# Two blocks on one core: merged activations turned by VectorE, low splits on GpSimd, memory rows scaled later

## The reference, cut to what matters

```python
merged = sigmoid(g_ret) * (o_ret @ w_ret_up) + sigmoid(g_moba) * (o_moba @ w_moba_up)
x = x + merged @ w_out
...
mkv = rms_norm(mem, mem_norm_g) @ w_mem_kv
...
merged = jnp.einsum('bsnd,bsnd->bsd', g, y_br)
x = x + merged @ w_out_2
```

## Time and profile before

| | |
|---|---|
| median of 3 runs | 2433.71 us (2433.43 to 2434.93) |
| the profiled execution, whole | 2433.67 us |
| its span, first to last instruction | 2431.8 us |
| PE busy | 2423.5 us, 100% of the span |
| PEld busy | 2000.7 us, 82% |
| DVE busy | 1682.1 us, 69% |
| ACT busy | 1241.7 us, 51% |
| POOL busy | 239.3 us, 10% |
| DMA | 464.20 MB, mean 191 GB/s |

### The profile page before, as it was taken

How to read it: one execution, slowest core, us unless ns; L and a number is a source line. 1 busy time by engine, 2 the same in 40 slices (tenths; PEclk the granted TensorE clock), 3 DMA queues, 4 the chain that set the end, 5 groups by cost and what they waited for, 6 DMA issues and landing times.

```text
span 2431.8 us, 34053 instructions
## 1 busy us (share of the span) xinstructions
PE 2423.5 (100%) x11017; PEld 2000.7 (82%) x11017; DVE 1682.1 (69%) x2171; ACT 1241.7 (51%) x1620; POOL 239.3 (10%) x250
## 2 busy tenths in 40 slices
PE   9999999999999999999999999999999999999999
PEld 7888888878888888888888878888887888888887
DVE  5467655587877988988888887454456645587564
ACT  5445454555455444444444445454556555655443
POOL 0022233231000000000000000010101100521000
PEclk9999999999999999999999999999999999999999
DMA  7655555576655655555555656855554545555655
GB/s 269 192 189 173 183 175 179 190 223 227 208 191 173 205 192 193 193 192 192 188 192 196 198 183 210 252 185 169 173 184 158 181 164 174 180 167 171 226 182 164
DMA packets 134822, 464.20 MB, mean 191 GB/s; under 512 B 14544, under 2 KB 21328, under 8 KB 134112
## 3 DMA queue, kind: packets, MB, share of 16 engines
q1 hardware_dynamic: 122464, 443.08, 55.6%
q10 hardware_dynamic: 12256, 20.15, 2.5%
q0 software_dynamic: 32, 0.03, 0.0%
HBM read 455.87 MB, written 7.34 MB: 190 GB/s over the span
## 4 chain that ended last, share of the span: by engine, by line
PE 98%; DVE 1%; issue 1%; ACT 0%; ACTq 0%; DVEq 0%
PE PS L646 21%; PE PS L648 21%; PE PS L647 21%; PE PS L893 7%; PE PS L894 7%; PE PS L895 7%; PE PS L913 3%; PE PS L915 3%; PE PS L914 3%; PE PS L758 1%; PE PS L728 1%; PE PS L687 1%; PE PS L708 0%; PE PS L736 0%; DVE WL L1640 0%
## 5 line engine op out<-in xcount | busy, mean ns | idle before, releaser
L1640 DVE TENSOR_TENSOR WL<-RAW,WH 128x1024 fp32r<-128x1024 f32 x842 | 1058.4, 1261 | 702.3 <-ACT WH L1118 693.8
L1118 ACT ACTIVATE WH<-RAW 128x1024 fp32r<-128x1024 f32 x841 | 889.1, 1059 | 1098.9 <-PE PS L648 721.9
L646 PE MATMUL PS<-WH,HT 128*128 128x512 f32 (+1 forms) x1816 | 718.5, 396 | 0.2 <-DVE WL L1640 0.2
L648 PE MATMUL PS<-WH,HT 128*128 128x512 f32 (+1 forms) x1816 | 706.5, 389 | 0.0
L647 PE MATMUL PS<-WL,HT 128*128 128x512 f32 (+1 forms) x1816 | 705.5, 388 | 0.0
L646 PEld LDWEIGHTS PS<-WH,HT 128*128 128x128 f32 x1816 | 341.1, 188 | 72.6 <-issue 5.4
L648 PEld LDWEIGHTS PS<-WH,HT 128*128 128x128 f32 x1816 | 340.8, 188 | 70.9
L647 PEld LDWEIGHTS PS<-WL,HT 128*128 128x128 f32 x1816 | 341.3, 188 | 67.3
L893 PE MATMUL PS<-WH,HT 128*128 128x512 f32 x704 | 274.3, 390 | 0.0
L895 PE MATMUL PS<-WH,HT 128*128 128x512 f32 x704 | 273.9, 389 | 0.0
L894 PE MATMUL PS<-WL,HT 128*128 128x512 f32 x704 | 273.9, 389 | 0.0
(11 more groups left out here) (306 smaller groups left out, 2114.7 us busy)
## 6 DMA issues: line engine op xcount, KB each, us to landing
RAW<-w_stream SPq DMA_DIRECT2D x841, 512.0 KB, 3.3
bias_scratch<-BE ACTq DMA_DIRECT2D x12, 256.0 KB, 4.0
MEMR<-mem_in ACTq DMA_DIRECT2D x1, 2048.0 KB, 10.5
X<-x_in ACTq DMA_DIRECT2D x4, 512.0 KB, 4.4
x_scratch<-X ACTq DMA_DIRECT2D x4, 512.0 KB, 4.5
X<-x_scratch ACTq DMA_DIRECT2D x1, 2048.0 KB, 11.3
out<-X ACTq DMA_DIRECT2D x8, 256.0 KB, 3.0
X<-x_in SPq DMA_DIRECT2D x3, 512.0 KB, 9.6
```

The costliest lines, as they stand in the source:

```text
L646: pe.matmul(o, hi, WH[:, slot, kk, 0:cols], start=k == 0, stop=False)
L648: ins = pe.matmul(o, lo, WH[:, slot, kk, 0:cols], start=False, stop=k == nq * GK - 1)
L1118: act.activation(WH[:, g.slot(j)], RAW[:, g.slot(j)], ACT.Copy).then_inc(hi_split, 1)
L1640: dve.tensor_tensor(WL[:, s], RAW[:, s], WH[:, s].bitcast(F32), ALU.subtract).then_inc(lo_split, 1)
```

## The change

**Turning.** The 64 identity products on `MERGED1` and `MERGED2`, and the steps that made them, are gone from TensorE's program. VectorE turns each chunk of 4 tiles after its `up_chunk`, with 16 transposes of 32x256 from `MERGED` into a new SBUF tensor `MT` (`merged_turn`, semaphore `merged_turned`). ScalarE copies the high parts from `MT` (`merged_hi`: at steps 7, 11 and 15 of the up stage for chunks 0 to 2, at step 4 of the out stage for chunk 3, each behind that step's split), and VectorE subtracts the low parts from `MT` (`merged_lo`: those of chunk c-1 between `up_chunk(c)` and `merged_turn(c)`, those of chunk 3 at the end). TensorE waits before each of the first 8 groups of the out stage for the low parts of the two tiles that the group needs.

**Low splits.** In each of the two up stages VectorE makes the low parts of the groups 4 to 7 first and then none until its chunks are done. GpSimd makes those of the next 17 groups (8 to 24, counted from the stage's first group; 16 to 24 are the first nine of the out stage). VectorE waits for them and goes on with group 25.

**Memory rows.** They are turned unscaled. The inverse roots go to `XR[:, 2:4]` and are applied by ScalarE when it copies the products of `mem0`, `mem1` and `mem2` out of PSUM: two instructions of 128x512 in place of one of 128x1024. The squares move from step 3 to step 4 and write their unused output to PSUM. Turning and splitting move 2 steps later (6 to 21, and 22 to 29). `mem0` waits tile by tile.

The core of the diff:

```diff
+        MT = sb("MT", [P, KT, S], F32, at_u1)
+        POOL_SPLITS = NCH * GW + 5
...
-            rstd(2, norm_ms, norm_rstd, 2)
+            def low_splits(name, first, end):
+                g = At(GROUP0[name])
+                for j in range(first + RING, end + RING):
+                    hold(hi_split, g.count(j + 1))
+                    hold(lo_split, g.count(j))
+                    s = g.slot(j)
+                    pool.tensor_tensor(WL[:, s], RAW[:, s], WH[:, s].bitcast(F32), ALU.subtract).then_inc(lo_split, 1)
+
+            low_splits("up_ret", GW, POOL_SPLITS)
+            rstd(2, norm_ms, norm_rstd, 2, XR[:, 2:4])
...
+            low_splits("up_b", GW, POOL_SPLITS)
...
+            def turned(name):
 
                 def before(p):
-                    if p in (0, 6):
-                        pe.wait_ge(tr_lo, TR[name] + (12 if p == 0 else KT))
-                return steps, before
-            straight("up_ret", NCH, GW, U[0], up_steps("merged1", 0))
-            steps, before = out_steps("merged1", 0)
+                    if p < GD:
+                        pe.wait_ge(tr_lo, TR[name] + 2 * p + 2)
+                return before
+            straight("up_ret", NCH, GW, U[0])
+            pe.sem_inc(tr_done, KT)
...
-            straight("out1", NCH, GD, HT, steps, before)
-            pe.wait_ge(mem_lo, KT)
-            straight("mem0", 1, GD, MEMT, mem0_steps)
+            straight("out1", NCH, GD, HT, None, turned("merged1"))
+            straight("mem0", 1, GD, MEMT, mem0_steps, lambda p: pe.wait_ge(mem_lo, 2 * p + 2))
...
+            def merged_hi(name, chunks, c):
+                act.wait_ge(merged_turned, chunks + c + 1)
+                for k in range(FT * c, FT * c + FT):
+                    act.activation(HT[:, k, 0, :], MT[:, k], ACT.Copy).then_inc(tr_hi, 1)
+
             for p in range(NCH * GW):
                 split(At(GROUP0["up_ret"]), p + RING)
...
-                transposed("merged1", HT, merged_tiles(p), None)
-                if p == 3:
+                if p % GW == GW - 1 and p > GW:
+                    merged_hi("merged1", 0, p // GW - 1)
+                if p == 4:
                     act.wait_ge(mem_loaded, 16)
-                    for t in range(T):
-                        ins = act.activation(JUNK[:, t, :], MEMR[:, t, :], ACT.Square, scale=D ** -0.5, accum_out=MS[:, t:t + 1])
-                    ins.then_inc(norm_ms, 1)
+                    mean_squares([(MEMR[:, t, :], XR[:, 2 + t:3 + t]) for t in range(T)], D ** -0.5, norm_ms)
...
             for p in range(NCH * GD):
                 split(At(GROUP0["out1"]), p + RING)
-                if p in (1, 2):
-                    transposed("merged1", HT, merged_tiles(NCH * GW + p), None)
+                if p == 4:
+                    merged_hi("merged1", 0, NCH - 1)
...
+            def merged_turn(merged, chunks, c):
+
+                dve.wait_ge(merged_ready, chunks + c + 1)
+                for a in range(4):
+                    for b in range(4):
+                        src = merged[32 * a:32 * a + 32].rearrange("p t (k d) -> p t k d", k=KT)[:, :, FT * c:FT * c + FT, 32 * b:32 * b + 32]
+                        dst = MT[32 * b:32 * b + 32].rearrange("p k (t s) -> p t k s", t=T)[:, :, FT * c:FT * c + FT, 32 * a:32 * a + 32]
+                        ins = dve.transpose(dst, src)
+                ins.then_inc(merged_turned, 1)
+
+            def merged_lo(name, c):
+
+                for k in range(FT * c, FT * c + FT):
+                    dve.wait_ge(tr_hi, TR[name] + k + 1)
+                    dve.tensor_tensor(HT[:, k, 1, :], MT[:, k], HT[:, k, 0, :].bitcast(F32), ALU.subtract).then_inc(tr_lo, 1)
+
+            def merged_chunks(stage, name, chunks):
+
+                for p in range(GW):
+                    split(At(GROUP0[stage]), p + RING)
+                for c in range(NCH):
+                    up_chunk(stage, MERGED[name], c)
+                    if c:
+                        merged_lo(name, c - 1)
+                    merged_turn(MERGED[name], chunks, c)
+                merged_lo(name, NCH - 1)
+
             dve.wait_ge(prod_free, 2 + PROD0["up_ret"])
...
+            merged_chunks("up_ret", "merged1", 0)
+            dve.wait_ge(lo_split, GROUP0["up_ret"] + POOL_SPLITS + RING)
...
-            for p in range(NCH * GD):
+            dve.wait_ge(mem_loaded, 16)
+            for p in range(POOL_SPLITS - NCH * GW, NCH * GD):
                 split(At(GROUP0["out1"]), p + RING)
...
-                if 4 <= p < 20:
-                    dve.wait_ge(norm_rows, 1)
-                    turn_memory((p - 4) // 4, (p - 4) % 4)
+                if 6 <= p < 22:
+                    turn_memory((p - 6) // 4, (p - 6) % 4)
```

More of the change, by code:

```diff
@@ L321, in build @@
         mem_turned = sem("mem_turned")
+        merged_turned = sem("merged_turned")
         mem_hi = sem("mem_hi")
@@ L1085, in _ @@
             pe.wait_ge(head_out, HEADS + 1)
[L1086 to L1088 removed]
+            straight("up_b", NCH, GW, U[2])
+            straight("out2", NCH - 1, GD, HT, None, turned("merged2"))
             g, n = At(GROUP0["out2"]), At(PROD0["out2"] + NCH - 1)
@@ L1150, in project @@
                         split(g, p + RING)
-                        evacuations(name, g, i, p, 2, dst, func, name in ("moba_proj", "ret_proj", "gates_ret"))
+                        evacuations(name, g, i, p, 2, dst, func, XR[:, 0:T] if name in ("moba_proj", "ret_proj", "gates_ret") else None)
                         if steps:
@@ L1372, in _ @@
                 g = At(GROUP0["mem0"])
-                evacuations("mem0", g, 0, p, 1, lambda c: CKV[:, :, c:c + CH])
+                if p == GD - 1:
+                    act.wait_ge(norm_rstd, 2)
+                evacuations("mem0", g, 0, p, 1, lambda c: CKV[:, :, c:c + CH], ACT.Copy, XR[:, 2:4])
                 split(g, p + RING)
@@ L1614, in _ @@
                 split(At(GROUP0["up_b"]), p + RING)
-                transposed("merged2", HT, merged_tiles(p), None)
+                if p % GW == GW - 1 and p > GW:
+                    merged_hi("merged2", NCH, p // GW - 1)
             for p in range(NCH * GD):
@@ L1891, in up_chunk @@
                 dve.tensor_tensor(merged[:, :, cols], merged[:, :, cols], gated, ALU.add).then_inc(merged_ready, 1)
-            dve.wait_ge(prod_free, 2 + PROD0["up_ret"])
[L1894 to L1898, removed]
-                if p in (8, 12):
-                    dve.wait_ge(norm_rstd, 2)
-                    ins = scaled_rows(MEMR, MEMR, p // 4 - 2)
-                    if p == 12:
-                        ins.then_inc(norm_rows, 1)
+            def merged_turn(merged, chunks, c):
[19 more added lines that the diff above has]
+                merged_lo(name, NCH - 1)
+            dve.wait_ge(prod_free, 2 + PROD0["up_ret"])
+            merged_chunks("up_ret", "merged1", 0)
+            dve.wait_ge(lo_split, GROUP0["up_ret"] + POOL_SPLITS + RING)
             def residual(name, p):
@@ L2187, in _ @@
             dve.wait_ge(prod_free, 2 + PROD0["up_b"])
-            for p in range(NCH * GW):
-                split(At(GROUP0["up_b"]), p + RING)
-                transposed("merged2", HT, merged_tiles(p), None)
-                if p % GW == GW - 1:
-                    up_chunk("up_b", MERGED["merged2"], p // GW)
+            merged_chunks("up_b", "merged2", NCH)
+            dve.wait_ge(lo_split, GROUP0["up_b"] + POOL_SPLITS + RING)
             dve.wait_ge(x_back, 16)
-            for p in range(NCH * GD):
+            for p in range(POOL_SPLITS - NCH * GW, NCH * GD):
                 if p + RING < NCH * GD:
                     split(At(GROUP0["out2"]), p + RING)
-                if p in (1, 2):
-                    transposed("merged2", HT, merged_tiles(NCH * GW + p), None)
                 if p == NCH * GD - 1:
```

50 lines of the change are left out of this document (16 added, 34 removed).

## The result

The changed kernel took **2472.13 us** (median of 4 runs, 2471.19 to 2472.88), the kernel before 2434.32 beside it (2433.43 to 2435.18): ratio 1.0155, 95% interval 1.0142 to 1.0167. That is 37.8 us slower, where 13.7 slower was forecast. The profiled execution took 2471.19 us, its span 2469.0.

What follows compares the result with a forecast made beforehand. TensorE, busy 2423.5 of 2431.8 us, was taken as the bound. 2433.67 - 7.7 (identity products gone) + 21.4 (waits, 10.7 per stage) = 2447.4 us; range 2425 to 2458.

Steps and rivals of the forecast that it cites:

- TensorE's 16 sets: Removing 64 identity products, in 16 sets of four at 0.48 us, takes 7.7 us from TensorE.
- VectorE's and GpSimd's durations: Up stages: 0.45 us per VectorE transpose; GpSimd subtraction 2.40 us plus gap 0.18, pace 2.58 us.
- That the two exclude each other: Up stages: VectorE operations with two SBUF inputs and GpSimd's exclude each other whole; TensorE waits 10.7 us per stage.
- A second slips into GpSimd's gap: Chunk 1's second low part runs without waiting; first and third wait 2.3 us each, with the addition 5.8 us.
- one low part per GpSimd operation: Rival, chance 0.10: each low part meets one GpSimd operation; 20.1 us per stage, 2466.2 us in total.
- the 1.2 of tile 12: Last chunk: the low part of tile 12 meets half a GpSimd operation, 1.2 us.
- 3.3 us to spare: Per stage, tiles 12 and 13 take 34.8 us; TensorE needs them after 38.1 us, leaving 3.3 us.
- the forecast's own case: Main forecast, chance 0.42: TensorE waits 10.7 us per stage, 2447.4 us in total, own range 2438 to 2454.
- GpSimd runs dry for a time; I count one wait less: Chunks 2 and 3: late high splits leave GpSimd without work, so meetings cost 3.5 us each.
- the additions' mean: Up stages: VectorE's additions to `MERGED` would show a mean of 2.4 us, far above 1.23.
- The clock: Rival, chance 0.10: TensorE's clock falls in two waits per stage, 2 us each, half lost; +4, 2451.4 us.
- The costs at nothing: `MEMR` scalings, scaled memory evictions, later turning and GpSimd's pace, among others, were taken to cost TensorE nothing.

Runs made afterwards that it cites:

- the kernels stand at 2426.86 and 2428.04: Changed kernel with low parts reading one PSUM input (real low parts left out), 2426.86 us; changed kernel with VectorE's transposes written to PSUM banks, 2428.04 us.
- the gap experiments: Changed kernel with extra semaphore increments before each of GpSimd's 34 subtractions: six, 2448.18 us and again 2446.51 us; one, 2454.62 us.
- The single increment: Changed kernel with one extra semaphore increment before each of GpSimd's subtractions: 2454.62 us.
- the kernel with these parts alone: Changed kernel with only GpSimd's low splits and the memory rows' part kept, TensorE turning as before: 2435.29 us, ratio 1.0002.
- one low part per chunk: Changed kernel with the four low parts of a chunk made by one VectorE instruction of 128x1024: 2442.26 us, ratio 1.0030.
- six increments: Changed kernel with six extra semaphore increments before each of GpSimd's subtractions: 2448.18 us, and 2446.51 us when run again.
- the turning alone: Changed kernel with VectorE keeping all low splits and GpSimd idle: 2472.80 us, ratio 1.0155.
- the filled kernel: Changed kernel with 16 matmuls into an unused PSUM bank at out groups 0, 4 and 6 of both out stages: 2468.19 us.

## Why the prediction was wrong, step by step

- **TensorE's 16 sets** at 0.48 us: right. Without new waits the kernels stand at 2426.86 and 2428.04, which is 8.1 and 6.8 under the kernel before beside them, where 7.7 was forecast.
- **VectorE's and GpSimd's durations**: right (0.436 us for 0.45 per transpose; 2.40 and a gap of 0.18 as forecast). The estimate of 2.25 us from the Trainium skill's "GPSIMD Engine Reference" was low: the trace has 2.40.
- **That the two exclude each other**: right, and with the clock the whole cause. The Trainium skill, "SBUF — State Buffer", section "SBUF: two separate sides", says of a VectorE operation with two SBUF inputs and a GpSimd operation that reads SBUF that whichever starts first gets the shared port pair for its whole instruction, and the other is blocked; the starts at 619.61 and 619.64 and the gap experiments agree.
- **"A second slips into GpSimd's gap": this step failed.** No row showed a second short VectorE operation starting inside a gap of 0.18 us; the earlier trace rows show a GpSimd operation going first. The trace of the changed kernel shows GpSimd 0.03 us ahead wherever it had work. So the chunks of the first stage cost 9.4 (0.6 at the addition, 8.8 at the low parts), 6.5 and 6.5 us of meetings instead of 5.8, 3.5 and 3.5; in the second stage the addition's share is 1.4. The last chunk's low parts, counted with 1.2, met nothing (1.43 us for four). These are nearly the terms of the rival "one low part per GpSimd operation", given 0.10. It forecast 20.1 us per stage; the waits and the slow matmuls ahead of the last wait come to 14.9 + 5.1 = 20.0 in the first and 17.3 + 3.5 = 20.8 in the second. That the rival comes out to 1 us is luck in part: its 6.5 for the later chunks was not worked out (its own 10.4 less one wait of 2.3 is 8.1), it left out the 1.2 of tile 12, and chunk 1 started 1.3 us later than the 3.3 us to spare assume, because VectorE was still turning chunk 0. The single increment built the forecast's own case: there they come to 11.1 and 11.9, against 10.7 forecast. The price of a meeting was right; their number was wrong.
- **"GpSimd runs dry for a time; I count one wait less"**: it did run dry (7.40 us), and this saved the addition's meeting and the first low part's, which started at 616.80, before GpSimd's 616.96: 9.4 - 6.5 = 2.9 us. The credit was about right; the other three low parts still met one operation each. The forecast of 2.4 us as the additions' mean was too high: it is 1370 ns in the first stage.
- **The clock** was a rival at 0.10, and came on top. It fell after each of six waits of 4.2 to 6.0 us. The distances are 0.43 us, not the 0.47 taken from the earlier trace rows, where the 4.21 us hold the whole duration of the ninth matmul. What is lost behind the last waits, 4.1 us in both stages together, was forecast as 4, but from two waits per stage of 2 us each with half of it lost; there were three, and a third of 12.8 us was lost. That the two numbers agree is luck. By the rule in the Trainium skill's "TensorE: Matmul & The Clock Gate", section "HAM oscillation — how this bites in real kernels", TensorE comes back at half clock from too long an idle time; the trace agrees, now in mid-run, in all six waits of 4.2 us and more. Together: 2433.67 - 7.7 + 20.0 + 20.8 + 4.1 = 2470.9, as in the account above.
- **The costs at nothing**: right for the scalings, the scaled evictions and GpSimd's pace, shown by the kernel with these parts alone.

The rival that came true was priced near the truth, but at 0.10 and outside the range, and the rivals stood as alternatives: the case in which two hold at once was nowhere.

## What to carry to other kernels

Beside a GpSimd that works without pause, count how many VectorE operations with two SBUF inputs there are before how long they are: each can cost a whole GpSimd operation, 2.5 us here for one of 0.42. Put one operand in PSUM (a transpose can write there at 456 instead of 436 ns), or merge the short ones into one. And look at what queues behind a wait on a third engine: ScalarE, standing for the turned tiles, held up GpSimd's input and set up the next meeting.

## What the runs showed of the hardware that was not expected

- The order of the two engines at the shared resource is decided by 0.03 us, and 0.08 us of delay on GpSimd is worth 17.5 us here.
- A block transpose of 32x256 from SBUF takes 436 ns to SBUF and 456 to PSUM, and isn't touched by GpSimd's subtractions: it takes the same 436 in the kernel in which GpSimd idles.
- The clock stayed up behind single waits of 2.4 and 2.5 us and was down at the restart, or soon after it, behind nearly all of 3.2 us and longer. Behind 3.2 us (one low part per chunk), 3.7 (six increments), 5.0 and 4.3 (the turning alone) the first matmuls still came at the upper clock, and the distance went to 0.43 us only 0.6 to 1.4 us after the restart. Two waits of 3.2 us in the filled kernel differ: the clock fell 0.8 us after one (restart at 2379.21), and stayed up through the 12 matmuls behind the other (637.45), to be down after the next wait, of 2.2 us.
- One execution of the kernel with six increments took 8391.33 us, the others 2446.13 to 2448.74. In its profile TensorE's matmuls start 0.84 us apart in most places looked at (0.62 near 8000 us), while its granted clock is given as 1.00, and VectorE's split and ScalarE's copy keep their 1228 and 1057 ns. It did not come back in the other eight executions of this kernel, and its cause is open.
